# A decoder step with pooling and sparse attention: where the prompt's compression and the conditioning sums stand in TensorE's order

## What is computed

```python
def _in_proj(x, c, norm_w, w_ada, b_ada, w_in):
    ada = jax.nn.silu(c) @ w_ada + b_ada
    shift, scale, gate = jnp.split(ada, 3, axis=-1)
    h = _rmsnorm(x, norm_w) * (1.0 + scale[:, None, :]) + shift[:, None, :]
    z = h @ w_in
    ...
def _compress(kv, w1, pe, w2):
    ch = kv.reshape(B, n_str, CMP_STRIDE, 2, KV_HEADS, HEAD_DIM)
    pre = 0.0
    for m in range(span):
        sl = slice(m * CMP_STRIDE, (m + 1) * CMP_STRIDE)
        a = jnp.einsum('bnjkgd,jkdh->bnkgh', ch, w1[sl]) + jnp.einsum('jkd,jkdh->kh', pe[sl], w1[sl])[:, None, :]
        pre = pre + a[:, m:m + n_cmp]
    comp = jnp.einsum('bnkgh,khd->bnkgd', jax.nn.gelu(pre), w2)
```

## Time and profile before

| what | value |
|---|---|
| median of 3 runs | 841.26 us (840.94 to 841.51) |
| the profiled execution, its own time | 840.98 us |
| its span, first to last instruction | 839.2 us |
| mean granted clock of PE | 0.952 |
| PE busy | 757.2 us, 90% of the span |
| DVE, ACT, POOL busy | 421.1, 288.4, 109.5 us |

### The profile page before, as it was taken

One profiled execution on the slowest core, in us unless ns is written; L12 is line 12 of the kernel. 1 busy time (PEld: TensorE's weight loads), 2 busy tenths in 40 slices (PEclk: granted clock), 3 DMA queues, 4 the chain that ended last, 5 costly groups with the idle time before them and its releaser, 6 DMA issues.

```text
span 839.2 us, 15317 instructions
## 1 busy us (share of the span) xinstructions
PE 757.2 (90%) x6221; PEld 551.6 (66%) x6221; DVE 421.1 (50%) x934; ACT 288.4 (34%) x772; POOL 109.5 (13%) x178
## 2 busy tenths in 40 slices
PE   0889899999979997999969899899999999869995
PEld 0847799999975776965556556566776677635441
DVE  0746468888871255003265666664545454243432
ACT  0326334444450001000046566562334434362211
POOL 2300330000000000000078212111111111000000
PEclk9999989999999998699969999999999999869998
DMA  9996913333000322020076700002476674410121
GB/s 242 347 346 228 397 54 151 151 151 151 1 0 1 93 79 84 1 83 1 2 258 270 288 1 2 1 2 89 168 250 228 219 241 155 178 61 1 53 86 37
DMA packets 37529, 108.08 MB, mean 129 GB/s; under 512 B 5716, under 2 KB 21123, under 8 KB 36308
## 3 DMA queue, kind: packets, MB, share of 16 engines
q1 hardware_dynamic: 31699, 56.77, 20.2%
q0 software_dynamic: 5760, 50.33, 16.2%
HBM read 101.80 MB, written 11.55 MB: 135 GB/s over the span
## 4 chain that ended last, share of the span: by engine, by line
PE 78%; DVE 8%; DMA 5%; SPq 3%; ACT 3%; issue 2%; POOL 1%; ACTq 0%; DVEq 0%; POOLq 0%
PE ps L901 13%; PE ps L1371 8%; PE ps L1068 8%; PE ps L1066 7%; PE ps L1217 5%; DMA wcols<-in_w_ada 5%; PE ps L878 4%; PE ps L1122 3%; PE ps L1171 3%; PE ps L1298 3%; PE ps L1282 2%; PE ps L1146 2%; PE ps L1230 2%; SPq L674 2%; PE ps L1035 2%
## 5 line engine op out<-in xcount | busy, mean ns | idle before, releaser
L901 PE MATMUL ps<-xd,w 128*128 128x192 f32 (+1 forms) x512 | 94.3, 328 | 0.0
L901 PEld LDWEIGHTS ps<-xd,w 128*128 128x128 f32 x512 | 86.0, 193 | 0.0
L878 PE MATMUL ps<-ident,cache 128*128 128x128 f32 x384 | 55.3, 282 | 19.9 <-DMA w<-in_phi_w 19.0
L1371 PE MATMUL ps<-w_o,mixT 128*128 128x512 f32 (+1 forms) x160 | 70.1, 597 | 0.0
L1068 PE MATMUL ps<-wcols,hT 128*128 128x384 f32 (+1 forms) x192 | 66.9, 508 | 2.2 <-issue 2.2
L1217 PE MATMUL ps<-zw,hT 128*128 128x256 f32 x256 | 63.5, 388 | 3.1 <-ACT z_gate L1605 2.2
L878 PEld LDWEIGHTS ps<-ident,cache 128*128 128x128 f32 x384 | 47.3, 147 | 25.8 <-issue 23.2
L1066 PE MATMUL ps<-hT,wcols 128*128 128x288 f32 x256 | 63.1, 409 | 0.0
L1381 ACT COPY xt<-ps 64x384 f32<-64x384 f32 x64 | 30.2, 472 | 90.1 <-PE ps L878 89.9
L1066 PEld LDWEIGHTS ps<-hT,wcols 128*128 128x128 f32 x256 | 48.9, 192 | 13.7 <-issue 0.3
L1911 DVE TENSOR_REDUCE peak<-ps 128x2 f32<-128x256 f32 (+3 forms) x48 | 39.5, 823 | 35.0 <-PE ps L1125 34.9
(11 more groups left out here) (314 smaller groups left out, 1192.6 us busy)
## 6 DMA issues: line engine op xcount, KB each, us to landing
wcols<-in_w_ada SPq DMA_DIRECT2D x6, 2048.0 KB, 10.9
win_rows<-in_state_win_kv SPq DMA_DIRECT2D x8, 768.0 KB
out<-in_state_win_kv SPq DMA_DIRECT2D x1, 6048.0 KB
zw<-in_w_in SPq DMA_DIRECT2D x4, 1024.0 KB, 6.0
wcols<-in_w_in SPq DMA_DIRECT2D x2, 1536.0 KB, 11.0
w_o<-in_w_out SPq DMA_DIRECT2D x1, 3072.0 KB, 11.5
w<-in_phi_w SPq DMA_DIRECT2D x4, 512.0 KB, 8.7
x_rows<-in_x_prompt SPq DMA_DIRECT2D x1, 2048.0 KB, 15.9
```

What stands on the lines that cost most here:

```text
L878: last = pe.transpose(ps[:, (2 * n + j) % 3, c * P:(c + 1) * P], caches[b % 2][:, 2 * s + j, c * P:(c + 1) * P], ident[:])
L901: last = pe.matmul(out, w[:, k, :], x[:, k * G:(k + 1) * G, 0:width], start=(s == 0 and k == 0), stop=(s == JP - 1), skip_group_check=True)
L1371: last = pe.matmul(ps[0:rows, 3 + n % 2 * 2 + half, :], mixT[n % 2][:, c, 0:rows], w_o[c // 6][:, c % 6, half * 512:(half + 1) * 512], sta ...
```

## The change

`xp_job` becomes 19, so `compress_prompt`, and the copies that belong to it on ACT and DVE, stand behind jobs 17 and 18 (front and back of the first 128 columns of `u`) and ahead of jobs 19 and 20. The banks of the ring and of the hidden sums move along, as they are counted from `xp_job`: the ring gets banks 3 to 7 and 0, the sums get banks 1 and 2, which jobs 17 and 18 used. In place of one wait for all earlier jobs' copies, each of the first six transposes waits for the copy of the job that used its own bank last (jobs 11 to 16), and the hidden sums wait for the copies of jobs 17 and 18.

`turn_ada` gets a part number: 8 of its 24 products run ahead of each of steps 18, 19 and 20, and the last part raises `ada_turned`.

```diff
--- before.py
+++ after.py
@@ -262,7 +262,7 @@
         block_jobs = [sum(1 for j in jobs if j[0] <= n) for n in range(len(IN_BLOCKS))]
         first_job = [0] + block_jobs
         XP_BLOCK = 3
-        xp_job = first_job[XP_BLOCK]
+        xp_job = first_job[XP_BLOCK] + 2
         CMP_JOB = first_job[4]
         job_bank = [j % 8 if j < CMP_JOB else (j - CMP_JOB) % 6 for j in range(len(jobs))]
         job_before = [max((k for k in range(j) if job_bank[k] == job_bank[j]), default=None) for j in range(len(jobs))]
@@ -844,13 +844,14 @@
                                      start=(c < 4), stop=(c >= KC - 4))
                 last.then_inc(ada_used, 1)
 
-            def turn_ada():
+            def turn_ada(part):
 
                 pe.wait_ge(ada_copied, n_ada)
-                for c in range(3 * KC):
+                for c in range(part * KC, (part + 1) * KC):
                     m = G * d + c * NB
                     last = pe.matmul(ps[:, 7, m:m + NB], ada_rows[:, c * P:(c + 1) * P], sel_ada[:], start=True, stop=True)
-                last.then_inc(ada_turned, 1)
+                if part == 2:
+                    last.then_inc(ada_turned, 1)
 
             def second_layer(b):
 
@@ -933,8 +934,8 @@
                 b, s = divmod(n, JP)
                 if n in ADA_AT:
                     ada_block(ADA_AT[n])
-                if n == ADA_TURN:
-                    turn_ada()
+                if ADA_TURN <= n < ADA_TURN + 3:
+                    turn_ada(n - ADA_TURN)
                 turn_step(n)
                 if n > JP:
                     add_step(n - 1)
@@ -1017,16 +1018,19 @@
             def compress_prompt():
 
                 pe.wait_ge(xp_in, 16)
-                for e in range(2):
-                    pe.wait_ge(job_out[e], max(by[j][1] for j in range(xp_job) if by[j][0] == e))
                 for s in range(JP):
                     for j in range(2):
                         if s >= 3:
                             pe.wait_ge(xp_out[j], s - 2)
+                        else:
+                            k = xp_job + 2 * s + j - 8
+                            pe.wait_ge(job_out[by[k][0]], by[k][1])
                         for c in range(KV // P):
                             last = pe.transpose(ps[:, xp_bank[s % 3][j], c * PSTR:(c + 1) * PSTR],
                                                 xp[:, 2 * s + j, c * P:(c + 1) * P], ident[0:PSTR, 0:PSTR])
                         last.then_inc(xp_turned, 1)
+                for k in range(xp_job - 2, xp_job):
+                    pe.wait_ge(job_out[by[k][0]], by[k][1])
                 for c in range(JP):
                     for e in range(2):
                         pe.wait_ge(xp_out[e], c + 1)
```

## The result

| what | before | after |
|---|---|---|
| median of 4 runs each, taken side by side | 841.1 us (840.44 to 841.51) | 832.66 us (831.76 to 834.67) |
| the profiled execution (its span) | 840.98 us (839.2) | 832.70 us (830.9) |
| mean granted clock of PE | 0.952 | 0.962 |

The ratio is 0.9902, with a 95% interval of 0.9886 to 0.9918: 8.2 us less, 6.9 to 9.6. The forecast was 830.8, so the gain is 2 us smaller than forecast.

The account below looks back on a forecast made before the run. PE, ending the chain for 78% of the span, was taken to bound the kernel through idling and half clock. From 840.98, 5.1 (part 1) and 5.4 (part 2) came off: 830.5, on the median 830.8 us; range 822.0 to 834.5.

Parts of the forecast that it names:

- What bounds the kernel: Whole kernel: PE ends the chain for 78% of the span and loses time by idling or half clock.
- Part 1, the mechanism: Conditioning sums in three parts: clock 1.00 over the parts and steps 18 to 20, step 19 starting near 105.7.
- Part 1, the size: Conditioning sums in three parts: 2.1 us gained in the burst and 3.0 behind it, sum 5.1 us.
- Part 2: Compression behind jobs 17 and 18: 4.2 us idling gone, 1.2 off the transposes, hidden sums still 13.75 us; gain 5.4.
- the two small terms that I let cancel: Compression: hidden sums partly fast, at most 1.2 us gained; slow clock reaching further into job 19, at most 1.5 lost.
- rival B: Compression: the clock stays up, hidden sums take 6.9 us, 7.4 us more gained, 823.4 us; chance 0.24.
- C: Conditioning steps: DVE stuck behind POOL's scaling, 3.4 us of part 1 lost, 834.2 us; sign: DVE operations over 1 us; chance 0.05.
- D: Compression: the wait only shifts, PE idles 4.2 us for another copy or load, 835.0 us; chance 0.05.
- E: Conditioning sums: first part lowers the clock, which stays low until the third is done; +7.8 us, 843.7 us; chance 0.03.

Follow-up runs that it names:

- the one with the waits alone: Kernel before with only the waits by bank; compression stays ahead of job 17, sums in one burst: 838.52 us, ratio 0.9962.
- the one with the compression alone: Changed kernel with the conditioning sums back in one burst at step 18; compression still moved, waits by bank: 836.06 us, ratio 0.9931.
- the kernel with the sums alone: Kernel before with only the conditioning sums in three parts, the compression where it was: 837.75 us, ratio 0.9961.
- two parts: Changed kernel with the conditioning sums in two parts of 24 matmul records, ahead of steps 18 and 19: 835.57 us, ratio 0.9927.
- one wait: Changed kernel with one wait for all earlier jobs' copies ahead of the transposes in place of the waits by bank: 833.41 us, ratio 0.9898.
- the pair of fillers: Changed kernel plus a 256-column product after each of eight transposing steps: on 32 rows 838.53 us, ratio 0.9969; on 128 rows 829.87 us, ratio 0.9872.

## Why the prediction was right, and where it missed

**What bounds the kernel**: right. PE's idling and its slow clock account for the gain in the two places; no other engine and no DMA took their place.

**Part 1, the mechanism**: right at each sign named. Clock 1.00 over the parts and steps 18 to 20, step 19's transposes 6.04 us behind the first part's start (101.04 to 107.08; 6.03 forecast, from the same start).

**Part 1, the size**: this is the term that was sized too high. In the two profiled executions the 5.1 is indeed found (-5.06), but it was read from one execution of before, and that one had the longest fall of the three bursts that were profiled. At full clock the burst and step 18 would take 3 x 1.73 + 2.57 = 7.76 us. Three profiled executions have the single burst, and took 12.46 (and 0.4 more behind it), 11.23 and 9.56 us for it: the kernel before, the one with the waits alone, the one with the compression alone. So the loss was 5.1, 3.5 and 1.8 us for the same instructions, 3.5 in the mean, and the kernel with the sums alone gained 3.3. The stretch from the sums to job 16's small copies agrees: it took 224.84, 223.21 and 222.83 us in these three, and 219.62 to 221.12 in the eight profiles with three parts (mean 220.58), so 3.05 less in the mean; the pair before and after stands near the far ends of both. With 3.3 in place of 5.1 the sum is 841.3 - 3.3 - 5.4 = 832.6, and the median is 832.66; so good an agreement is partly luck, as the intervals are over 1 us on each side. The forecast's other assumption, that everything behind comes earlier by the same amount, left room for a microsecond or two, and that was needed: +1.49 behind job 21. The pair before and after alone would even put the whole shortfall outside the two places, as -5.06 and -6.13 are 11.2 where 10.5 was forecast; it is the other profiles and the kernel with the sums alone that put it into part 1.

**Part 2**: right. The 4.21 us of idling are gone. The transposes took 3.90 where the pace of the copies gave 4.05. In this profile the fall came 1.7 us into the hidden sums and not near the transposes' end, so the two small terms that I let cancel, at most 1.2 gained and at most 1.5 lost, were 1.53 gained, more than the bound, and 0.94 lost. In the three other profiles with the compression in this place (it alone, two parts, one wait) the fall came 0.6 to 1.5 us ahead of the hidden sums, as forecast, and these took 13.76 us. In sum 6.1 in the two profiles and 5.8 (3.4 to 8.2) with this part alone, for 5.4.

**The choice between forecast and rival B**, which I named as the likeliest to be wrong, went by the nearest row: that 32 rows behave like the 9-row matmuls of the earlier trace rows and not like its 128-row transposes. It came out right, but one of its two rows was read too short. The first row ends at 249.8. Behind it, in the kernel before:

```profile
249.90:252.00 2.10, 0.00 (x0) 0.00 (x0) 2.03 (x7) 0.61 (x2) 0.00 (x0) 1.00 0.00 0
252.90:256.20 3.30, 3.30 (x7) 1.77 (x6) 0.00 (x0) 0.00 (x0) 0.00 (x0) 0.50 0.02 5
```

PE idles for 2.2 us, and then the clock is at 0.50 here too, as it is near this place in every profile of this case. So these transposes don't show that 128 rows hold the clock, and what the prediction drew from them for rival B doesn't stand. What shows that rows matter is the pair of fillers. The Trainium skill's rule (TensorE: Matmul & The Clock Gate, Part 4: PE-mode transpose), that a PE transpose doesn't count for the gate as a matmul does, gave the same outcome as the forecast; the 128-row transposes, which the prediction held against it, don't count against it. The pair of fillers doesn't refute it either, but by that pair it isn't the whole: the 32-row product is no transpose and didn't keep the clock. Nor are rows the whole: the sums of 9 columns have all 128 rows, and the clock fell in their single burst.

**C** shows once and cost nothing that can be seen. Of the eight of DVE's differences that ran beside POOL's scaling in the changed kernel (99.70 to 114.22), one took 0.90 us, below the 1 us that was to be the sign, and seven took 0.54 to 0.56; the three steps' transposes follow one another at 4.34 and 4.33 us. Two of the eight (timeline):

```profile
104.85 0.56 DVE L1719 TENSOR_TENSOR xd<-xt 128x384 f32<-128x384 f32 x1
...
109.18 0.90 DVE L1719 TENSOR_TENSOR xd<-xt 128x384 f32<-128x384 f32 x1
```

**D** would have shown as idle time at 328.17, and there is none; with the waits alone, without the move, it does happen (3.25 us). **E** would have shown as 0.50 over the parts; they have 1.00. With parts of 24 records, though, the first half of what it supposes did happen: the clock fell behind the first part, and again behind the second. But the step between them lifted it.

**What stays open**: why the same burst lowers the clock for 3.4 us in one execution and 10.2 in another. No run here separates its moment from what went before it. And what the falls behind job 21 cost, which differ from execution to execution, I didn't measure; +1.49 is the sum of all that lies there in one pair of profiles.

## What to carry to other kernels

Read PE's granted clock like an idle time, and look at what stands *behind* a fall: here 4 us of thin transposes cost little by themselves, and 5 us by making the hidden sums behind them run at half rate (12.22 us for 7.2), which came back when the transposes were spread among products of 128 rows, or had such products put between them. Where a wait is moved off, ask whose queue it really was (DVE's sixteen small copies here): finer waits alone left 3.25 of 4.21 us. And size a term of the clock by several executions, not by the one whose profile is at hand.

## What the runs showed of the hardware that I had not expected

- The hidden sums didn't raise the clock, and kept it where they followed work on 128 rows: entered at 1.00 behind such work they kept it for all of their 7.1 us (three kernels); entered at 0.50 they stayed there for 13.7 us (the kernel before and others). In the changed kernel, right behind the thin transposes, they were entered at 1.00, lost it after 1.7 us and stayed at 0.50 for 10.4. The products of 288 columns behind them, job 17 before and job 19 after, had it back after 1.0 and 3.1 us.
- Being busy is not enough: 32-row transposes without a gap (PE 3.20 of 3.20 us, PEld 3.17) were followed by 0.50, and so were the same transposes with 256-column products on 32 rows between them, while with such products on 128 rows, PEld at 6.08 of 8.80 us, the clock stayed at 1.00.
- The kernel before's executions, as far as the ratios count them, spread over 838.2 to 844.2 us. And falls come at different moments and with different lengths in code that is the same: 10.2, 6.8 and 3.4 us in the profiles of the three kernels with the single burst.
